# Attention scores from high and low parts, and one filling tile behind every head

## Chip, core and metric

The kernel runs on one core of one Trainium2 chip. The time is the device time of one execution in microseconds (us). Five engines work side by side and meet at semaphores: PE (TensorE: matmul; its weight loads are listed as PEld), DVE (VectorE), ACT (ScalarE), POOL (GpSimd) and SP (SyncE), which here issues the loads of the weights.

## What is computed

Four layers over 512 positions of width 1024, all in float32. Layers 0 and 1 are a retention and convolution block with a feed-forward part; the change does not touch what they do. Layers 2 and 3 are the second block, and the change is in its latent attention:

```python
def mla_attention(c_q, c_kv, k_rope_in, q_norm_g, w_uq, kv_norm_g, w_ukv):
    q = (rmsnorm_2(c_q, q_norm_g) @ w_uq).reshape(B, S, H, 192)      # 8 heads: 128 + 64 rotated
    kv = (rmsnorm_2(c_kv, kv_norm_g) @ w_ukv).reshape(B, S, H, 256)  # keys 128, values 128
    q_nope, q_rope = q[..., :128], rope(q[..., 128:])
    k_nope, v = kv[..., :128], kv[..., 128:]
    k_rope = rope(k_rope_in)                                         # one for all heads
    ...
    s = einsum('bqhd,bkhd->bhqk', qi, k) * scale                     # blocks of 128 queries
    s = where(key_chunk <= q_chunk, s, -1e30)
    p = softmax(s)
    return einsum('bhqk,bkhd->bqhd', p, v)
```

Around it, `y_b = mla_attention(...) * silu(z_b)`, and `merged` is the sum of `sigmoid(g) * (y @ w_proj)` over three branches, of which attention is b.

## The kernel before

A weight chunk, mostly 128 x 1024, is loaded by SP into one of four buffers (`raw`), ACT casts it to fp32r as the high part (L896), and DVE subtracts to get the low part (L1313); `slot(name)` on ACT and DVE cuts the chunk that stands two behind `name` in the list made by `plan()`. A product with a weight is then three fp32r matmuls (`three`: high x high, high x low, low x high), and a `tile` is eight such triples of 512 columns, so 24 matmuls into one of eight PSUM banks. Most of the kernel is such tiles. All matmuls are issued by the helper `mm`, line 448, so the views tell them apart by their operands: `h`, `r` are fp32r tiles in the arena, `wh`, `wl` the parts of a weight, `f` are float32 tiles, `ct` the constants.

Each engine has a program of its own, in `build`, and runs it in order. In `mixer2(L)` (L = 2, 3) PE's order is: the tiles ckv1, kr, zb0, the rotation of the keys (`rotate(L, 4)`), zb1, zb2; the rotated channels of the queries, qr0 and qr1, with the rotations between; the values vb0 and vb1; and then the heads. Small steps (`BESIDE`) are tied to the slots of ckv1 and the four chunks behind it: the two norms of the latent vectors. `heads(h)` makes the query part qn (9 matmuls) and the key part kn (6) of head h and then one filling tile: zb3 to zb7 for h = 0 to 4, none for h = 5, gateb_0 and gateb_1 for h = 6 and 7 (these two keep their banks until the projection of branch b). The order written out is

```python
heads(0); scores(0)
for h in range(8):
    if h < 7: heads(h + 1)
    turn(h)                  # ten transposes of the probabilities
    if h < 7: scores(h + 1)
    values(h)
```

`scores(h)` works in float32: for i = 0 to 3 the 128 queries of block i against 128 (i + 1) keys, one matmul over the 128 plain channels and one over the 64 rotated ones (upper or lower half of the partitions by the head). ACT copies qn out of PSUM (`copied`, L977) and DVE kn (L1687), two buffers each. Behind the scores DVE masks (L1700), takes the maximum (L1702), ACT takes the exponentials (L1167), DVE scales (L1712); PE turns the probabilities (L795), ACT (L1177) and DVE (L1720) copy them, and `values(h)` multiplies in float32. DVE multiplies by the gate (L1727), ACT and DVE split the result (L970, L1323). The rotation is POOL's (`cosine` L1921, `roped` L1926) and DVE's (`rotated` L1537). Behind the heads come the v tiles (va, 192 matmuls) and the projection of branch b with its gates (`gate_proj`).

Of the kernel before, what the change touches and what calls it, by code (L numbers as in the profile page):

```python
# [43 lines left out]
def plan():  # L44
# [43 lines left out]
    for l in range(2):  # L88
# [10 lines left out]
        for h in range(3):  # L99
            one("zb", D2["zb"], h)  # L100
# [6 lines left out]
        for h in range(8):  # L107
            out.append((f"{L}/qk{h}", [("mla_w_uq_2", l, k * P, P, rng(h * 192)) for k in range(3)]
                        + [("mla_w_ukv_2", l, k * P, P, rng(h * 256)) for k in range(2)]))
            if h < 5:  # L110
                one("zb", D2["zb"], h + 3)
            elif h > 5:
                one("gateb_", D2["gate"] + 1024, h - 6)

        def proj(nm, w, nk, b):
            if nm != "b":
                one(f"gate{nm}_", D2["gate"] + 1024 * b, 0)
            for j in range(8):
                if j < 7 and (nm, j) != ("b", 0):
                    one(f"gate{nm}_", D2["gate"] + 1024 * b, j + 1)  # L120
# [69 lines left out]
ZB_AT = (20, 21, 22, 23, 29, 30, 31, 67)  # L190
# [122 lines left out]
ROPE_T = {0: (64, 65, 66, 67), 1: (64, 65, 66, 68, 57)}  # L313
# [6 lines left out]
def build(nc, x_in, wst, vec, cst, tab, gmb, gains_in, out):  # L320
    ctx = ExitStack()
    with ctx:
# [52 lines left out]
        def turned(key):  # L375
            return bank(key).rearrange("p (k s) -> p k s", k=4)

# [57 lines left out]
        def tensor(e, w):  # L435
# [292 lines left out]
            def mixer2(L):  # L728
# [6 lines left out]
                tile(f"{L}/zb2", xs)  # L735
# [26 lines left out]
                def heads(h):  # L762
# [6 lines left out]
                    if h < 5:  # L769
                        tile(f"{L}/zb{h + 3}", xs)  # L770
                    elif h > 5:
                        tile(f"{L}/gateb_{h - 6}", xs, hold=True)

                def scores(h):
                    part = slice(64 * (h % 2), 64 * (h % 2) + 64)
                    qn, kn = F(55 + 2 * (h % 2)), F(56 + 2 * (h % 2))
                    w.wait_ge(*at("qn", L, h))
                    w.wait_ge(*at("kn", L, h))
                    w.wait_ge(*at("roped", L, 3))
                    w.wait_ge(*at("roped", L, 4))  # L780
                    for i in range(NT):
                        n = (i + 1) * P
                        o = take(("s", L, h, i))
                        mm(o[:, 0:n], qn[:, i * P:n], kn[:, 0:n], True, False)
                        mm(o[:, 0:n], F(43 + h // 2)[part, i * P:n], F(42)[part, 0:n], False, True).then_inc(
# [22 lines left out]

                heads(0)
                scores(0)  # L810
                for h in range(8):
                    if h < 7:
                        heads(h + 1)
                    turn(h)
                    if h < 7:
                        scores(h + 1)
                    values(h)
# [17 lines left out]
                banks.let_go(f"{L}/gateb_0")  # L835
                banks.let_go(f"{L}/gateb_1")
                gate_proj(L, "b", "b", "b", pair(16, 24, 8), ("b_lo", L), first=2)
# [44 lines left out]
        def scalar(e, w):  # L882
# [144 lines left out]
            def gate_proj(L, b, g, p, first=0, kind="one", cut_merged=None):  # L1027
                if first == 0:
                    slot(f"{L}/gate{g}_0")
                ring = (66, 67, 68) if L < 2 else (46, 47, 48) if b == "b" else (64, 65, 66)  # L1030
                for j in range(8):
# [6 lines left out]
                    key = f"{L}/gate{g}_{j}"  # L1038
                    w.wait_ge(*at("done", key))
# [1132 lines left out]
```

## Time and profile before

| | |
|---|---|
| three timed runs | 3335.03, 3328.9, 3334.95 us |
| their median | 3334.95 us |
| the profiled execution | 3340.64 us |
| its span, first to last instruction | 3339.3 us |
| PE busy | 3287.9 us (98%) |
| DVE, ACT, POOL busy | 1797.3, 1211.4, 374.6 us |
| mean granted TensorE clock | 0.992 |

Times in rows are from the span's start. Matmuls overlap in the pipeline, so their listed durations are longer than the pace at which they come; the pace is read from the starts. A float32 matmul shows as two instructions, an fp32r one as one. The first scores of layer 2 start at 1772.59 us, and its v tiles at 1915.85; in layer 3 these are 2596.8 and 2741.6.

### The profile page before, as it was taken

Reading aid. Unit: us, or ns where it says so; the run is one execution under the profiler, and the core shown is the slowest. Engines: PE = TensorE matmul, PEld = TensorE weight load, DVE = VectorE, ACT = ScalarE, POOL = GpSimd, SP = SyncE. Lnnn points to the kernel's source line nnn. Section 1 sums busy time; section 2 is a strip of 40 time slices with the busy share of each in tenths; the row PEclk is TensorE's granted clock in tenths of the full one; section 3 lists DMA queues with packets and bytes.
Section 4 is the critical chain, followed back from the end, with each engine's and each line's share of the span. In section 5 each row is a group of like instructions: output and inputs, shape, how many; then the busy total and the mean of one; then the engine's idle time right before and its main releaser. Section 6 shows DMA issues by size and latency. Waiting matters only on the chain.

```text
span 3339.3 us, 36641 instructions
## 1 busy us (share of the span) xinstructions
PE 3287.9 (98%) x14952; PEld 2674.4 (80%) x14952; DVE 1797.3 (54%) x2349; ACT 1211.4 (36%) x1800; POOL 374.6 (11%) x292
## 2 busy tenths in 40 slices
PE   8999999999999999999999999999999999999999
PEld 7788888888878888788886588888888668888887
DVE  4785556665478455666554443447554444344754
ACT  3232334444323233334443322236534322223742
POOL 1111211110111111111020000110012000011001
PEclk9999999999999999999999899999999989999999
DMA  4223222245322322324521132223232122222232
GB/s 157 70 81 103 95 95 95 95 146 189 121 69 80 104 90 93 101 95 148 190 92 49 63 102 88 95 88 98 92 123 78 53 69 89 94 95 90 86 104 96
DMA packets 93638, 330.84 MB, mean 99 GB/s; under 512 B 10560, under 2 KB 10816, under 8 KB 92704
## 3 DMA queue, kind: packets, MB, share of 16 engines
q1 hardware_dynamic: 90144, 313.90, 28.0%
q0 software_dynamic: 3328, 14.59, 1.3%
q8 instruction: 120, 1.97, 0.2%
q14 instruction: 46, 0.38, 0.0%
HBM read 326.35 MB, written 2.10 MB: 98 GB/s over the span
## 4 chain that ended last, share of the span: by engine, by line
PE 94%; DVE 3%; ACT 1%; issue 1%; POOL 0%; DMA 0%; SPq 0%; ACTq 0%; DVEq 0%; POOLq 0%
PE ps L448 93%; DVE wl L1313 1%; ACT wh L896 1%; PE ps L553 1%; PE ps L795 0%; DVE f L1607 0%; DVE X L1423 0%; DMA raw<-wst 0%; ACT f L1167 0%; ACT r L970 0%; DVE f L1420 0%; DVE f L1367 0%; POOL f L1985 0%; DVE f L1712 0%; DVE f L1432 0%
## 5 line engine op out<-in xcount | busy, mean ns | idle before, releaser
L448 PE MATMUL ps<-h,wh 128*128 128x512 f32 (+1 forms) x5824 | 1711.2, 378 | 11.9 <-issue 7.5
L448 PEld LDWEIGHTS ps<-h,wh 128*128 128x128 f32 x5824 | 1070.7, 189 | 213.7 <-issue 19.6
L448 PE MATMUL ps<-h,wl 128*128 128x512 f32 (+1 forms) x2912 | 1095.8, 376 | 0.0
L1313 DVE TENSOR_TENSOR wl<-raw,wh 128x1024 fp32r<-128x1024 f32 (+3 forms) x592 | 740.5, 1265 | 377.7 <-ACT wh L896 376.5
L896 ACT CAST wh<-raw 128x1024 fp32r<-128x1024 f32 (+3 forms) x596 | 593.7, 1009 | 735.5 <-PE ps L448 726.1
L448 PEld LDWEIGHTS ps<-h,wl 128*128 128x128 f32 x2912 | 551.1, 189 | 99.9
L448 PE MATMUL ps<-r,wh 128*128 128x512 f32 x1632 | 506.8, 392 | 1.2 <-DVE f L1367 1.2
L448 PEld LDWEIGHTS ps<-r,wh 128*128 128x128 f32 x1632 | 305.1, 188 | 68.5 <-issue 6.4
L448 PE MATMUL ps<-r,wl 128*128 128x512 f32 x816 | 317.8, 389 | 0.0
L448 PE MATMUL ps<-wh,r 128*128 128x512 f32 x960 | 304.7, 392 | 0.3
L970 ACT CAST r<-f 128x512 fp32r<-128x512 f32 x182 | 111.9, 620 | 515.4 <-DVE f L1616 145.9
L1524 DVE TENSOR_TENSOR f<-f,ps 128x512 f32<-128x512 f32 x96 | 65.9, 686 | 386.6 <-PE ps L448 384.3
L448 PEld LDWEIGHTS ps<-wh,r 128*128 128x128 f32 x960 | 180.2, 188 | 39.9 <-ACT r L896 1.9
L448 PE MATMUL ps<-f,f 128*128 128x128 f32 (+7 forms) x640 | 201.8, 450 | 7.6 <-DVE f L1687 4.3
L1955 POOL TENSOR_TENSOR f<-f,f 128x512 f32<-128x512 f32 x64 | 114.4, 1790 | 752.4 <-DVE f L1524 752.4
L448 PEld LDWEIGHTS ps<-f,f 128*128 128x128 f32 (+1 forms) x640 | 106.2, 198 | 105.8 <-issue 80.1
L448 PE MATMUL ps<-wl,r 128*128 128x512 f32 x480 | 186.8, 389 | 0.0
L1323 DVE TENSOR_TENSOR r<-f,r 128x512 fp32r<-128x512 f32 x182 | 124.6, 690 | 115.5 <-ACT r L970 115.4
L448 PEld LDWEIGHTS ps<-r,wl 128*128 128x128 f32 x816 | 153.1, 188 | 32.2
L1337 DVE SCALAR_TENSOR_TENSOR f<-f,vt,f 128x511 f32<-128x511 f32 (+29 forms) x240 | 174.5, 788 | 0.0
L1607 DVE SCALAR_TENSOR_TENSOR f<-ps,vt,f 128x511 f32<-128x511 f32 (+1 forms) x176 | 131.2, 747 | 64.3 <-ACT f L1104 61.2
L448 PE MATMUL ps<-wh,h 128*128 128x512 f32 x384 | 122.3, 397 | 0.0
(142 smaller groups left out, 2133.7 us busy)
## 6 DMA issues: line engine op xcount, KB each, us to landing
raw<-wst SPq DMA_DIRECT2D x544, 512.0 KB, 3.3
raw<-wst SPq DMA_DIRECT2D x48, 320.0 KB, 3.0
f<-gains POOLq DMA_DIRECT2D x6, 1024.0 KB, 5.2
raw<-wst SPq DMA_DIRECT2D x16, 384.0 KB, 3.1
f<-tab POOLq DMA_DIRECT2D x16, 256.0 KB, 4.2
X<-x_in SPq DMA_DIRECT2D x4, 512.0 KB, 7.7
f<-gmb POOLq DMA_DIRECT2D x4, 512.0 KB, 4.6
raw<-wst SPq DMA_DIRECT2D x8, 256.0 KB, 2.9
```

The lines of the kernel that those rows point to most:

```text
L448: return e.matmul(o, a, b, start=start, stop=stop, skip_group_check=True)
L553: last = e.transpose(o[:, i * P:(i + 1) * P], F(H[a])[:, i * P:(i + 1) * P], ident)
L896: e.copy(h[:, 0:WIDTH[c]], raw[:, c % NRAW, 0:WIDTH[c]]).then_inc(*hi_cut.up(("hi", c)))
L970: e.copy(r, f).then_inc(*act_hi.up(event))
L1313: e.tensor_tensor(l[:, 0:WIDTH[c]], raw[:, c % NRAW, 0:WIDTH[c]], h[:, 0:WIDTH[c]].bitcast(F32), ALU.subtract).then_inc(*lo_cut.up(("lo", c)))
L1323: e.tensor_tensor(lo, f, hi.bitcast(F32), ALU.subtract).then_inc(*dve_lo.up(event))
L1337: e.scalar_tensor_tensor(out=C, in0=F(16 + j)[:, 0:S - s], scalar=vec1(L, "cfw", 31 * j + i)[:, 0:1], in1=C, op0=ALU.mult, op1=ALU.add).th ...
L1524: e.tensor_tensor(F(M + j) if begins else q, q, bank(key), ALU.mult).then_inc(*dve_tile.up(("free", key), *events))
L1607: e.scalar_tensor_tensor(out=q[:, s:S], in0=bank(key)[:, 0:S - s], scalar=vec1(L, "fcw", 3 * (22 * m + j) + 2 - s)[:, 0:1], in1=q[:, s:S], ...
L1955: e.tensor_tensor(F(M + j), F(M + j), F(ring[j % 3]), ALU.add).then_inc(*pool_sum.up(*events))
```

## The change

- The scores: ACT casts qn and kn to fp32r (55 and 57), DVE subtracts for the low parts (56 and 58), one buffer each. For the plain channels PE does `three`. The rotated queries of a head are kept with the high part in the head's own 64 partitions and the low part in the other 64 of one tile; the rotated keys have the same 64 channels in both halves, so one matmul over 128 rows gives high x high and low x high, and one over 64 rows gives high x low. Five fp32r matmuls take the place of two float32 ones.
- ACT and DVE split the rotated parts: one cast and one subtraction for the keys, two each of 64 partitions for every one of the four query tiles. POOL leaves the rotated result in place.
- The filling tiles: zb2 leaves the place ahead of the queries, heads 0 to 4 are followed by zb2 to zb6, heads 5 to 7 by gateb_0 to gateb_2, and zb7 is split: six of its eight triples ahead of the last turning and two ahead of the last values. ACT takes the sigmoid of gateb_0 at head 5. The norm's last step moves with its slot to qr0.

The diff, cut to its core (the same moves of zb and gateb chunks in `plan()` and in each engine's program left out):

```diff
-ZB_AT = (20, 21, 22, 23, 29, 30, 31, 67)
+ZB_AT = (17, 26, 19, 28, 29, 30, 31, 67)
+QR_AT = ((43, 16), (44, 18), (45, 20), (46, 22))
+KR_AT = (42, 23)
...
 # tensor, mixer2
                 for p in range(2):
+                    slot(f"{L}/qr{p}")
                     h, l = weights(f"{L}/qr{p}")
...
                     if h < 5:
-                        tile(f"{L}/zb{h + 3}", xs)
-                    elif h > 5:
-                        tile(f"{L}/gateb_{h - 6}", xs, hold=True)
+                        tile(f"{L}/zb{h + 2}", xs)
+                    else:
+                        tile(f"{L}/gateb_{h - 5}", xs, hold=h > 5)
...
                 def scores(h):
                     part = slice(64 * (h % 2), 64 * (h % 2) + 64)
-                    qn, kn = F(55 + 2 * (h % 2)), F(56 + 2 * (h % 2))
+                    qr, (kr_h, kr_l) = R(QR_AT[h // 2][h % 2]), (R(i) for i in KR_AT)
                     w.wait_ge(*at("qn", L, h))
                     w.wait_ge(*at("kn", L, h))
-                    w.wait_ge(*at("roped", L, 3))
-                    w.wait_ge(*at("roped", L, 4))
+                    w.wait_ge(*at("rope_lo", L, 4, 0))
+                    w.wait_ge(*at("rope_lo", L, h // 2, h % 2))
                     for i in range(NT):
                         n = (i + 1) * P
+                        b = slice(i * P, n)
                         o = take(("s", L, h, i))
-                        mm(o[:, 0:n], qn[:, i * P:n], kn[:, 0:n], True, False)
-                        mm(o[:, 0:n], F(43 + h // 2)[part, i * P:n], F(42)[part, 0:n], False, True).then_inc(
+                        three(o[:, 0:n], R(55)[:, b], R(56)[:, b], R(57)[:, 0:n], R(58)[:, 0:n], True, False)
+                        mm(o[:, 0:n], qr[:, b], kr_h[:, 0:n], False, False)
+                        mm(o[:, 0:n], qr[part, b], kr_l[part, 0:n], False, True).then_inc(
                             *group_done.up(("done", ("s", L, h, i))))
...
+                def last_gate(some):
+                    name = f"{L}/zb7"
+                    h, l = weights(name)
+                    if some[0] == 0:
+                        take(name)
+                    last = group(bank(name), h, l, [k * P for k in some], [xs[k] for k in some], some[0] == 0, some[-1] == 7)
+                    if some[-1] == 7:
+                        last.then_inc(*group_done.up(("done", name), ("closed", NAME[name])))
...
                 for h in range(8):
                     if h < 7:
                         heads(h + 1)
+                    else:
+                        last_gate(range(0, 6))
                     turn(h)
                     if h < 7:
                         scores(h + 1)
+                    else:
+                        last_gate(range(6, 8))
                     values(h)
 # scalar, mixer2
+                def rope_hi(r):
+                    w.wait_ge(*at("roped", L, r))
+                    t = F(ROPE_T[1][r])
+                    if r == 4:
+                        e.copy(R(KR_AT[0]), t).then_inc(*act_hi.up(("rope_hi", L, 4, 0)))
+                        return
+                    for m in range(2):
+                        part = slice(64 * m, 64 * m + 64)
+                        e.copy(R(QR_AT[r][m])[part, :], t[part, :]).then_inc(*act_hi.up(("rope_hi", L, r, m)))
...
                 def heads(h):
                     slot(f"{L}/qk{h}")
-                    more = (at("done", ("s", L, h - 2, 3)),) if h > 1 else ()
-                    copied(("qn", L, h), F(55 + 2 * (h % 2)), ("qn", L, h), *more)
+                    more = (at("done", ("s", L, h - 1, 3)),) if h else ()
+                    hi_part(bank(("qn", L, h)), R(55), at("done", ("qn", L, h)), ("qn_hi", L, h), *more)
+                    hi_part(bank(("kn", L, h)), R(57), at("done", ("kn", L, h)), ("kn_hi", L, h))
...
+                    if h == 5:
+                        key = f"{L}/gateb_0"
+                        w.wait_ge(*at("done", key))
+                        e.activation(gate_at(L, "b", 0), bank(key), ACT.Sigmoid).then_inc(
+                            *act_tile.up(("gate", L, "b", 0), ("free", key)))
 # vector, mixer2
+                def rope_lo(r):
+                    t = F(ROPE_T[1][r])
+                    if r == 4:
+                        lo_part(t, R(KR_AT[0]), R(KR_AT[1]), at("rope_hi", L, 4, 0), ("rope_lo", L, 4, 0))
+                        return
+                    for m in range(2):
+                        part, other = slice(64 * m, 64 * m + 64), slice(64 - 64 * m, 128 - 64 * m)
+                        q = R(QR_AT[r][m])
+                        lo_part(t[part, :], q[part, :], q[other, :], at("rope_hi", L, r, m), ("rope_lo", L, r, m))
...
                 def heads(h):
                     slot(f"{L}/qk{h}")
-                    key = ("kn", L, h)
-                    w.wait_ge(*at("done", key))
-                    if h > 1:
-                        w.wait_ge(*at("done", ("s", L, h - 2, 3)))
-                    e.tensor_copy(F(56 + 2 * (h % 2)), bank(key)).then_inc(*dve_tile.up(("kn", L, h), ("free", key)))
+                    for nm, hi in (("qn", 55), ("kn", 57)):
+                        key = (nm, L, h)
+                        w.wait_ge(*at(nm + "_hi", L, h))
+                        e.tensor_tensor(R(hi + 1), bank(key), R(hi).bitcast(F32), ALU.subtract).then_inc(
+                            *dve_lo.up((nm, L, h), ("free", key)))
...
 # gpsimd
             def roped(L, r, dst):
...
-                e.tensor_tensor(F(dst), F(dst), F(ROPE_T[L // 2][r]), ALU.add).then_inc(*pool_tile.up(("roped", L, r)))
+                t = F(ROPE_T[L // 2][r])
+                e.tensor_tensor(F(dst) if L < 2 else t, F(dst), t, ALU.add).then_inc(*pool_tile.up(("roped", L, r)))
```

On ACT, `rope_hi(4)` stands in the query loop behind the slot of qr1, and `rope_hi` of query tiles 0 and 1 behind the copies of vb0, of 2 and 3 behind those of vb1; on DVE `rope_lo` likewise.

## Rows read from the trace of the kernel before

**Rows 1.** The page's fourth part: the chain that ended last, by engine.

```profile
PE 94%; DVE 3%; ACT 1%; issue 1%; POOL 0%; DMA 0%; SPq 0%; ACTq 0%; DVEq 0%; POOLq 0%
```

**Rows 2.** Windows: length, then PE, PEld, DVE, ACT, POOL busy, granted clock, DMA.

```profile
1741.12:1763.74 22.62, 22.62 (x93) 17.28 (x92) 7.86 (x9) 10.41 (x16) 11.71 (x8) 1.00 0.22 75
1806.42:1824.42 18.00, 18.00 (x75) 12.09 (x74) 9.21 (x22) 6.28 (x16) 0.00 (x0) 1.00 0.16 48
1857.30:1870.18 12.88, 12.88 (x24) 5.18 (x25) 3.25 (x12) 2.14 (x8) 0.00 (x0) 0.60 0.12 41
1907.98:1911.59 3.61, 1.90 (x10) 1.19 (x11) 2.83 (x6) 1.38 (x3) 0.00 (x0) 0.85 0.65 263
1911.59:1915.85 4.26, 4.26 (x8) 2.44 (x9) 0.00 (x0) 0.00 (x0) 0.00 (x0) 0.50 0.01 4
1915.85:1960.16 44.31, 44.31 (x194) 36.65 (x194) 11.27 (x11) 12.71 (x16) 0.00 (x0) 0.98 0.30 95
2681.50:2695.97 14.47, 14.47 (x25) 5.94 (x25) 3.49 (x13) 2.15 (x8) 0.00 (x0) 0.53 0.11 36
```

**Rows 3.** Timeline of PE: start, length, operation; the first score block and one head.

```profile
1772.59 5.84 PE L448 MATMUL ps<-f,f 128*128 128x128 f32 x16
1778.36 0.73 PE L448 MATMUL ps<-r,wh 128*128 128x512 f32 x2
...
1805.34 1.25 PE L795 MATMUL ps<-ct,f 128*128 128x128 f32 x10
1806.42 8.20 PE L448 MATMUL ps<-f,f 128*128 128x128 f32 x24
1814.38 0.70 PE L448 MATMUL ps<-r,wh 128*128 128x512 f32 x2
```

**Rows 4.** PE's waits, 1709 to 1987 us: who for whom, total, times, longest.

```profile
PE ps L448 <- DVE f L1687: 2.2, 1, 2.2
PE ps L448 <- DVE f L1720: 1.6, 1, 1.6
PE ps L795 <- DVE f L1712: 1.5, 1, 1.5
```

**Rows 5.** Timeline of the weight loads: two changes of rows, then the values.

```profile
1789.78 0.29 PEld L448 LDWEIGHTS ps<-f,f 64*128 64x128 f32 x2 [0.33 <-issue]
...
1794.20 0.30 PEld L448 LDWEIGHTS ps<-f,f 128*128 128x128 f32 x2 [0.76 <-issue]
...
1795.17 1.27 PEld L448 LDWEIGHTS ps<-f,f 128*128 128x128 f32 x5 [0.24 <-issue]
```

**Rows 6.** Timeline of PE: fp32r matmuls of 256 and of 512 columns.

```profile
1707.49 0.40 PE L448 MATMUL ps<-h,wh 128*128 128x256 f32 x2
...
1707.85 0.40 PE L448 MATMUL ps<-h,wh 128*128 128x256 f32 x2
...
1758.08 0.62 PE L448 MATMUL ps<-wh,r 128*128 128x512 f32 x2
...
1758.76 0.62 PE L448 MATMUL ps<-wh,r 128*128 128x512 f32 x2
```

**Rows 7.** Timeline of the weight loads in layer 0: fp32r ahead of 64 rows.

```profile
120.86 0.19 PEld L448 LDWEIGHTS ps<-h,wl 128*128 128x128 f32 x1
121.40 0.29 PEld L448 LDWEIGHTS ps<-f,f 64*128 64x128 f32 x2 [0.35 <-issue]
```

**Rows 8.** Timeline of DVE behind a score block that ends at 1812.2.

```profile
1815.82 1.28 DVE L1712 TENSOR_SCALAR f<-f,sm 128x128 f32<-128x128 f32 x4
...
1818.38 0.69 DVE L1323 TENSOR_TENSOR r<-f,r 128x512 fp32r<-128x512 f32 x1 [0.69 <-ACT r L970]
...
1819.75 0.68 DVE L1687 COPY f<-ps 128x512 f32<-128x512 f32 x1
```

**Rows 9.** Timelines of ACT and of PE around the first rotation.

```profile
1737.95 1.28 ACT L970 CAST r<-f 128x512 fp32r<-128x512 f32 x2 [1.68 <-DVE f L1381]
...
1745.20 0.59 PE L448 MATMUL ps<-f,ct 128*128 128x512 f32 x1
```

More of the change, by code:

```diff
@@ L98, in plan @@
         out.append((f"{L}/kr", [(A, l, k * P, P, rng(D2["kr"], 64)) for k in range(8) for _ in range(2)]))
-        for h in range(3):
+        for h in range(2):
             one("zb", D2["zb"], h)
@@ L110, in plan @@
             if h < 5:
-                one("zb", D2["zb"], h + 3)
-            elif h > 5:
-                one("gateb_", D2["gate"] + 1024, h - 6)
+                one("zb", D2["zb"], h + 2)
+            else:
+                one("gateb_", D2["gate"] + 1024, h - 5)
+        one("zb", D2["zb"], 7)
         def proj(nm, w, nk, b):
@@ L118, in proj @@
             for j in range(8):
-                if j < 7 and (nm, j) != ("b", 0):
+                if j < 7 and (nm != "b" or j > 1):
                     one(f"gate{nm}_", D2["gate"] + 1024 * b, j + 1)
@@ L376, in turned, with gate_at @@
             return bank(key).rearrange("p (k s) -> p k s", k=4)
+        def gate_at(L, b, j):
+            if L < 2:
+                return F(66 + j % 3)
+            if b == "b":
+                return F(68 if j == 0 else 46 + j % 3)
+            return F(64 + j % 3)
         def stat(t):
@@ L834, in mixer2 @@
                                 last.then_inc(*group_done.up(*closes))
-                banks.let_go(f"{L}/gateb_0")
                 banks.let_go(f"{L}/gateb_1")
-                gate_proj(L, "b", "b", "b", pair(16, 24, 8), ("b_lo", L), first=2)
+                banks.let_go(f"{L}/gateb_2")
+                gate_proj(L, "b", "b", "b", pair(16, 24, 8), ("b_lo", L), first=3)
                 for nm in ("u", "za"):
@@ L1184, in mixer2 @@
                         heads(h + 1)
+                    else:
+                        slot(f"{L}/zb7")
                     turn(h)
@@ L1193, in mixer2 @@
                         copied(("va", L, n, t), F(32 + 2 * t, 2)[:, n * S:(n + 1) * S], ("va", L, n, t))
-                gate_proj(L, "b", "b", "b", first=2)
+                gate_proj(L, "b", "b", "b", first=3)
                 for nm in ("u", "za"):
@@ L1735, in mixer2 @@
                         heads(h + 1)
+                    else:
+                        slot(f"{L}/zb7")
                     turn(h)
@@ L1745, in mixer2 @@
                         slot(f"{L}/va{n_}_{c}")
-                gate_proj(L, "b", "b", "b", first=2)
+                gate_proj(L, "b", "b", "b", first=3)
                 for nm in ("u", "za"):
```

57 lines of the change are left out of this document (34 added, 23 removed).

## The prediction

> **What bounds the kernel now.** First the page's chain of work, which gives 94% of the span of 3339.3 us to PE [rows 1]. TensorE is nearly never without work, so only what shortens TensorE's own stream, or its few pauses, moves the end. The profiled execution took 3340.64 us (1.3 us lie outside its span); the three timed runs have a median of 3334.95 and reach from 3328.9 to 3335.03.
>
> Second, the timeline of PE in one attention stage. A head is one period: score matmuls, values, the projections of the next head, a filling tile, the turning of the probabilities; it lasts 18.00 us from one score block to the next [rows 2], with no pause. The first head's score block stands alone, from 1772.59 to 1778.36: 5.77 us. Scores and values together go from 1806.42 to 1814.38, 7.96 us, so values take 2.19; ten transposes take 1.09 (1805.34 to 1806.42) [rows 3].
>
> Third, PE's waits from 1709 to 1987 us. Three pauses of the stage stand there: 2.15 us before head 5's scores (until the copy of line 1687), 1.54 before the last head's turning (until the scaling of line 1712), 1.64 before its values (until the copy of line 1720) [rows 4]. They are the three places without a filling tile: heads(5) has none, and behind head 7 there is nothing left. The windows show what follows a pause: TensorE's granted clock is 1.00 in the ordinary head, a mean of 0.60 over the scores that follow the 2.15 us pause and 0.50 over the last values, which is the lower level, 1.2 GHz [rows 2].
>
> **The score block.** Before, each of a head's four score tiles (128, 256, 384, 512 columns, 1280 together) is two fp32 matmuls, one over 128 rows and one over 64; each shows as two instructions. After, it is five fp32r matmuls, four over 128 rows and one over 64. What does a column cost? The values are fp32 over 128 rows with the same 1280 columns and take 2.19 us with about 0.05 us of change at their ends, so two such sets stream for 4.27. The block takes 5.77, and 1.50 are left over for its eight changes between 128 and 64 rows: 0.19 each. The weight loads show the same: within the values the loads run on beneath the matmuls, while at each change the next load comes only after a gap of its own (0.33 us at 256 columns, 0.76 at 512), which is the streaming of the matmul before it and more [rows 5].
>
> An fp32r matmul of 512 columns comes every 0.227 us (three from 1758.08 to 1758.76), one of 256 columns every 0.120 (three from 1707.49 to 1707.85) [rows 6]. 384 columns lie between them: 0.174. For 128 columns no row shows fp32r. From below stands what the two widths extrapolate to, 0.067; from above the fp32 rate of four passes, 0.21. I take 0.112, since the transposes, which also load 128 columns of weights for each 128 streamed, come every 0.109 [rows 3]. Does the change from 128 to 64 rows also cost an fp32r stream? In layer 0 the last 128-row fp32r load starts at 120.86; at the pace of 0.227 the next would start at 121.09, beneath its matmul. That next one is of 64 rows and starts at 121.40 [rows 7]: the matmul has streamed its 512 columns by 121.30, and the load comes 0.1 us after that, uncovered. So I keep 0.19 for each of the eight changes; the bound below is zero (the load beneath the stream), the bound above 0.21 (0.1 of waiting and the 0.11 that the next load takes uncovered).
>
> New block: for each tile three steps at the sustained pace and two bare streams (before a change nothing is pushed on). 3 x (0.227 + 0.174 + 0.120 + 0.112) = 1.90; 2 x 1280 columns at 0.417 ns (2.13 us of the values over their 4 x 1280) = 1.07; 8 x 0.19 = 1.51. Sum 4.48 us against 5.77: 1.29 a head, **20.7 us** for 16 heads (two layers).
>
> The Trainium skill speaks for more: TensorE: Matmul & The Clock Gate, section "Step-by-step: what each phase is for", says that weight loads are pulled ahead of running matmuls if the row groups don't conflict or if they go to the background buffer. By it, a change of rows need cost nothing and the block would be 2.97 us, the whole gain 24 us larger. The trace agrees within one row count and not across a change [rows 5, 7].
>
> **The fillers.** Moving tiles changes no work: 24 matmuls each, before as after. zb2 goes from ahead of the queries to head 1, each later one a head on, gateb_0 to 2 behind heads 5 to 7, and zb7 is split 18 + 6 around the last turning. The pauses: 2.15 + 1.54 + 1.64 = 5.33 us a layer. What the lower clock adds in layer 2: scores and values of head 5 in 12.88 instead of 7.96 (4.92), the window of the last turning 3.61 less the pause of 1.64 at its end and the ordinary 1.09 (0.88), the last values 4.26 less 2.19 (2.07), the v stage 44.31 less 192 x 0.227 = 43.58 (0.73) [rows 2]: 8.60. In layer 3 the block of head 5 took 14.47 (6.51 over), 1.6 more: 10.2. Together 5.33 x 2 + 8.6 + 10.2 = **29.5 us**, if the fillers cover the pauses.
>
> Do they? From a score block's end (1812.2) its probabilities are ready at 1817.1 (four scalings, 1815.82 to 1817.10) [rows 8], 4.9 us. Behind heads 0 to 6 lie the values and, 18.00 - 7.96 - 1.09 = 8.95, the projections and a filler: 11.1. Behind head 7 lie 2.19 and 18 x 0.227 = 4.09: 6.3, enough. The last values then need the copies of line 1720: DVE has the product and the lower part of head 6 (1818.38 + 0.69, 6.9 us behind the block) and now also the cut of va0_1, 1.2; that and 0.7 for the copy give 9.0; PE arrives at 6.3 + 1.09 + 6 x 0.227 = 8.7. I charge **0.3 us** a layer.
>
> **New waits.** (1) Scores wait for low parts in place of copies: ACT casts two tiles a head (0.64 each, two in 1.28 [rows 9]) where it copied one, then DVE subtracts twice (0.69, as at 1818.38) where it copied once (0.68) [rows 8]. The copy of before ended at 1820.43 and the scores began at 1824.42: 4.0 us of room; the added 0.69, and up to 0.6 behind the second cast, leave 2.7. Queued behind are the next cut, the gate's product and the copy of the turned tile, all at least 2 us early. Cost nothing; without that cover up to 1.3 us a head. (2) The rope parts: nine casts and nine subtractions a layer, 0.6 to 0.7 each, about 6 us on ACT and on DVE, in the 22.6 us of the query and value projections, where ACT is busy for 10.4 and DVE for 7.9 [rows 2]. GpSimd writes in place, no more work. On ACT the last four stand ahead of head 0's casts; scores(0) come 8.8 us behind the last value tile (39 matmuls), and four casts, two more and two subtractions make 2.5 + 1.3 + 0.7, beside a cut of 1.0. Nothing. (3) With zb2 gone, TensorE reaches the first rotation one tile (5.5 us) sooner: at 1739.7, not 1745.2. That needs ACT's copy, which stands behind the two casts of the second norm, ended at 1739.23 [rows 9], pushed by a weight cut that is 1024 wide now and not 768 (0.2 to 0.4 more), and takes 0.6: 1740.2. PE waits **0.6 us** a layer; a bare queue of casts bounds it at 1.2, below at zero. (4) The sigmoid of gateb_0 stands among exponentials: ACT switches its table twice more a layer. ACT's idle time before head 5's exponentials covers both. Weight chunks stay in number; SP's queue has the same transfers in another order, TensorE consuming them 7% faster at the most; no PE wait in rows 4 is for a transfer.
>
> **Sum.** 20.7 + 29.5 - 2 x (0.3 + 0.6) = 48.4 us. Against the profiled time: 3340.6 - 48.4 = 3292.2; against the median: 3286.5. The profiled run was 5.7 above the median, and the length of the low-clock stretch differs between its own two layers by 1.6 us; part of that excess I expect to be what now goes away. I take **3288 us**.
>
> **Rivals.** A, 128 columns of fp32r run at the fp32 rate: five of them 1.07 instead of 0.44, 0.63 a head, 10 us: 3298. No row speaks against it. B, the loads at a change of rows run ahead once both sides are fp32r, and the change costs nothing: 1.51 a head more gained, 24 us: 3264. For it: within one row count every load is hidden [rows 5]; against it: an fp32r stream of 128 rows did not let the 64-row load ahead [rows 7]. (It is what the Trainium skill's rule above would give.) C, the clock falls in the new blocks: streaming is 2.67 of 4.48 us, before 4.27 of 5.77, so TensorE works less densely there, next to the turning. At 1.2 GHz such a block takes 2.7 us more; in half of the heads 21 us, 3310; in all, 3331, still not above before. For it: it fell after pauses in this very place; against it: no ordinary head shows it. D, a filler does not cover (the low parts arrive late in each head): 1.3 us a head and the pauses half kept, 3320. E, on the other side: fp32r with 64-row operands, or narrower than 512, is streamed at the fp32 rate in the score tiles altogether: five matmuls of four passes, 5 x 2.13 + 1.51 = 12.2 us a block, 6.4 more than before, 102 us: 3334.95 + 102 - 27.7 = 3409. It decides from a block of 7.5 us on (48.4 / 16 = 3.0 above 4.48). Against it: the 256-column rows. That the change does not do what it says would be D.
>
> **Chances.** Forecast 0.66, A 0.12, B 0.07, C 0.08 (3310), D 0.04, E 0.03. Range: 3264 to 3306 holds the forecast, A, B and the milder half of C; D, E, the rest of C and some 0.08 for sizes that I missed, 0.19 together, stay out. Within 0.2% (6.7 us) of before, which is about what a measurement of this kernel can tell from no change, lie only the ends of C and D: 0.02; slower: E and the unseen, 0.03; faster 0.95.
>
> **What would show it.** Period of a head 18.00 -> 16.7; the lone first block 5.77 -> 4.5; the loads at a change of rows still with a gap; no granted clock under 1.00 between the first scores and the v stage; PE's waits at lines 1687, 1712, 1720 gone, one of some 0.6 us for the ACT copy ahead of the first rotation and one of 0.3 ahead of the last values. A step under 0.1 us between the 128-column matmuls, or over 0.2, would correct the estimate; a low clock inside the heads would make the prediction wrong.

## The result, and the profile after

The changed kernel takes 3309.76 us, the median of four runs from 3306.52 to 3310.53; the kernel before beside it takes 3334.99 (3328.9 to 3337.31). The ratio is 0.9925, with a 95% interval of 0.9908 to 0.9942: faster by 25 us, where 47 were forecast. The forecast was 3288 with a range from 3264 to 3306; the time lies 3.8 us above the range. The direction was right, the size wrong. The profiled execution of the changed kernel took 3310.41 us.

The page of the kernel after, its head and its fourth part:

```profile
span 3309.1 us, 36837 instructions
PE 3258.3 (98%) x15016; PEld 2684.7 (81%) x15016; DVE 1820.3 (55%) x2383; ACT 1234.7 (37%) x1838; POOL 375.2 (11%) x292
...
PE 95%; DVE 2%; ACT 1%; issue 1%; POOL 0%; DMA 0%; SPq 0%; ACTq 0%; DVEq 0%; POOLq 0%
```

PE still sets the end, as in [rows 1]. Its waits from 1709 to 1987 us in the kernel after, in the columns of [rows 4]:

```profile
PE ps L461 <- issue: 4.6, 1, 4.6
PE ps L461 <- ACT f L1006: 0.9, 2, 0.5
```

The three pauses of [rows 4] are gone, and so is the lower clock behind them. In their place stands one pause of 4.6 us, more than any of the three, and its releaser is "issue": the profile names no one. Of the two waits for the ACT copy one (0.52 us) was there before, the other (0.42) is new. The timeline of PE shows where they stand: the first score block, one head, the new wait ahead of the first rotation, and the big pause.

```profile
1742.98 1.10 PE L461 MATMUL ps<-f,ct 128*128 128x512 f32 x2 [0.42 <-ACT f L1006]
...
1783.97 1.26 PE L810 MATMUL ps<-ct,f 128*128 128x128 f32 x10
1784.98 4.70 PE L461 MATMUL ps<-r,r 128*128 128x128 f32 x20
1789.61 2.42 PE L461 MATMUL ps<-f,f 128*128 128x512 f32 x8
1791.79 0.71 PE L461 MATMUL ps<-r,wh 128*128 128x512 f32 x2
...
1800.73 1.25 PE L810 MATMUL ps<-ct,f 128*128 128x128 f32 x10
...
1949.92 1.19 PE L461 MATMUL ps<-r,wh 128*128 128x512 f32 x2 [4.63 <-issue]
```

A head is now 16.76 us long (1783.97 to 1800.73) instead of 18.00; its score block takes 4.63 (1784.98 to 1789.61) instead of 5.77, its transposes 1.01 instead of 1.09. The pause ends at 1949.92, at the first matmul of branch b's projection (`gate_proj`), behind the v tiles. The windows of the kernel after, in the columns of [rows 2]: a head, the v tiles with the pause, and the first two tiles of the projection; then these last two again in layer 3.

```profile
1790.00:1806.77 16.77, 16.77 (x78) 12.84 (x77) 9.69 (x23) 6.77 (x16) 0.00 (x0) 1.00 0.16 51
1901.50:1949.92 48.42, 43.79 (x195) 35.98 (x194) 14.23 (x17) 17.07 (x21) 0.09 (x1) 0.98 0.28 91
1949.92:1963.43 13.51, 13.51 (x49) 10.90 (x49) 7.01 (x10) 1.05 (x1) 2.98 (x2) 0.80 0.18 64
...
2710.04:2758.49 48.45, 43.82 (x196) 35.97 (x194) 14.24 (x17) 17.07 (x21) 0.10 (x1) 0.99 0.28 91
2758.49:2772.19 13.70, 13.70 (x48) 11.03 (x49) 7.00 (x10) 1.05 (x1) 2.98 (x2) 0.79 0.18 64
```

The 48 matmuls behind the pause would take 48 x 0.227 = 10.9 us at the full clock; they take 13.5 and 13.7 at a mean granted clock of 0.80. The pause and what follows it cost (4.63 + 2.63) + (4.63 + 2.82) = 14.7 us. That alone carries most of the distance to the forecast. The question for the experiments is what PE waits for there.

What stands in front of PE's first projection matmul is its wait for a PSUM bank. The eight banks go round in a ring (`Banks.take`): each take gets the next bank that isn't held, and waits until the tile that had it is read ("free"). Counted through the code, take by take, in layer 2:

| take | before: bank, last tile in it | after: bank, last tile in it |
|---|---|---|
| held while the v tiles run | 1 (gateb_0), 5 (gateb_1) | 1 (gateb_1), 5 (gateb_2) |
| zb7, behind head 7 | none | 0 |
| last v tile | 7 | 0 |
| first projection tile, pr(b, 0) | 0, a v tile read long ago | 1, **gateb_1** |
| the next tile | 1, gateb_0 | 2, a v tile |

The held banks are let go just ahead of `gate_proj`. Before, the ring stood at bank 0 then. zb7 is one take more, the ring stands one bank further, and the first projection tile gets bank 1, which is free only when ACT has taken the sigmoid of gateb_1. ACT's timeline in the kernel after shows when:

```profile
1945.33 0.58 ACT L1006 COPY f<-ps 128x512 f32<-128x512 f32 x1 [0.77 <-PE ps L461]
1945.81 1.99 ACT L925 CAST wh<-raw 128x1024 fp32r<-128x1024 f32 x2
1947.82 1.28 ACT L1070 ACT_TABLE_LOAD   x1
1949.11 0.60 ACT L1070 ACTIVATE f<-ps 128x512 f32<-128x512 f32 x1
```

The sigmoid ends at 1949.71 and PE's next weight load starts at 1949.89. It stands behind the last copy of a v tile, two cuts of weight chunks (1.99) and a change of ACT's table (1.28). PE would have gone on at 1945.29.

A note on the table: the Trainium skill, ScalarE: Activation LUTs, section "What ACT_TABLE_LOAD costs", counts 1.28 us for the load and 1.38 more for a drain. The trace agrees with the first; of the second it shows nothing, since the cut ends 0.02 us before the load and the sigmoid starts 0.01 behind it. Read from the rows, the sigmoid in this place costs 1.9 us with its table.

### The profile page after: what moved, and what is told of

Its sections match the earlier page's. It is cut to its first block, busy times and chain, and to the rows that moved or that the text cites. A ratio compares the mean times of both kernels' runs of the same rounds, so it can differ in the third digit from the quotient of the medians.

```text
span 3309.1 us, 36837 instructions
## 1 busy us (share of the span) xinstructions
PE 3258.3 (98%) x15016; PEld 2684.7 (81%) x15016; DVE 1820.3 (55%) x2383; ACT 1234.7 (37%) x1838; POOL 375.2 (11%) x292
## 4 chain that ended last, share of the span: by engine, by line
PE 95%; DVE 2%; ACT 1%; issue 1%; POOL 0%; DMA 0%; SPq 0%; ACTq 0%; DVEq 0%; POOLq 0%
PE ps L461 94%; DVE wl L1367 1%; ACT wh L925 1%; PE ps L566 1%; PE ps L810 1%; DVE f L1661 0%; DVE X L1477 0%; DMA raw<-wst 0%; DVE f L1474 0%; DVE f L1421 0%; POOL f L2059 0%; DVE f L1486 0%; ACT r L999 0%; DVE f L1424 0%; ACT f L957 0%
## 5 line engine op out<-in xcount | busy, mean ns | idle before, releaser
L1377 DVE TENSOR_TENSOR r<-f,r 128x512 fp32r<-128x512 f32 (+1 forms) x200 | 140.7, 708 | 117.8 <-ACT r L999 115.4
L461 PE MATMUL ps<-r,r 128*128 128x512 f32 (+5 forms) x800 | 189.2, 376 | 0.0
L461 PEld LDWEIGHTS ps<-r,wl 128*128 128x128 f32 x816 | 154.3, 189 | 32.9
L461 PEld LDWEIGHTS ps<-r,r 128*128 128x128 f32 (+1 forms) x800 | 139.8, 188 | 39.4 <-issue 12.8
```

The costliest lines, as they stand in the source:

```text
L461: return e.matmul(o, a, b, start=start, stop=stop, skip_group_check=True)
L1377: e.tensor_tensor(lo, f, hi.bitcast(F32), ALU.subtract).then_inc(*dve_lo.up(event))
```

## Experiments

The theory: the pause is the bank, the lower clock follows from the pause, and the rest of the forecast holds. The rival: the pause belongs to the fp32r scores or their low parts, which keep DVE and ACT behind. Each kernel was timed beside the kernel before on the same chip; its median there is given in brackets.

### The held banks kept longer

In the changed kernel the two banks are let go two projection tiles later, so that pr(b, 0) takes a bank whose v tile has been read:

```diff
 # tensor, gate_proj
                 for j in range(8):
+                    if b == "b" and j == 2:
+                        banks.let_go(f"{L}/gateb_1")
+                        banks.let_go(f"{L}/gateb_2")
...
-                banks.let_go(f"{L}/gateb_1")
-                banks.let_go(f"{L}/gateb_2")
                 gate_proj(L, "b", "b", "b", pair(16, 24, 8), ("b_lo", L), first=3)
```

> The changed kernel with one difference: TensorE's program keeps the two held banks of gateb_1 and gateb_2 until the third projection of branch b, so the first projection takes a bank whose v tile was copied long before. Theory (bank): the 4.6 us pause behind the v tiles is the wait for the bank of gateb_1, which ACT's sigmoid frees; it goes, and with it the low clock behind it: v tiles 48.4 -> 43.6 us, the first three groups behind them 13.5 -> 10.9, 7.5 us a layer, about 15 in all, so some 3295 us. Rival (weights): the pause waits for the weight chunks of prb_0; it stays at 4.6 us and the time at 3310. Rival (clock moves on): the pause goes but the clock falls somewhere else near, and only 9.3 us come back: 3300.

Measured: 3295.14 us (before 3337.84), ratio 0.9871 [0.9856, 0.9886]. Windows of this kernel, the v tiles and the two projection tiles behind them, and its ACT timeline:

```profile
1901.13:1944.78 43.65, 43.65 (x195) 36.13 (x194) 11.28 (x11) 12.71 (x16) 0.00 (x0) 1.00 0.28 97
1944.78:1955.66 10.88, 10.88 (x49) 9.02 (x48) 8.51 (x14) 5.41 (x6) 1.54 (x1) 1.00 0.20 59
```
```profile
1945.46 1.99 ACT L926 CAST wh<-raw 128x1024 fp32r<-128x1024 f32 x2
1947.48 1.28 ACT L1071 ACT_TABLE_LOAD   x1
1948.77 0.60 ACT L1071 ACTIVATE f<-ps 128x512 f32<-128x512 f32 x1
```

ACT does exactly the same, and as late: its sigmoid ends at 1949.37, 4.6 us after PE has gone on at 1944.78. Nobody waits for it any more. The v tiles take 43.65, the tiles behind them 10.88, at a clock of 1.00, and no stretch of lower clock is left from about 1697 us to the last microseconds. 14.6 us against the changed kernel, with the same instructions in the same order and only other banks: the pause is the bank. The expectation's other rival, weight chunks that come late, falls too: ACT casts the same two chunks just as late, from 1945.46, and PE has gone on before.

### The sigmoid ahead of the cuts

The other way to release the bank sooner. On ACT, in `gate_proj` of branch b:

```diff
 # scalar, gate_proj
+                def gate(j):
+                    key = f"{L}/gate{g}_{j}"
...
+                    e.activation(gate_at(L, b, j), bank(key), ACT.Sigmoid).then_inc(
+                        *act_tile.up(("gate", L, b, j), ("free", key)))
+                if b == "b":
+                    gate(1)
                 for j in range(8):
...
-                    if (b, j) != ("b", 0):
...
+                    if (b, j) not in (("b", 0), ("b", 1)):
+                        gate(j)
```

> The changed kernel with one difference: ACT takes the sigmoid of gateb_1 ahead of the two weight cuts (1.05 us each) that stood before it. Theory (bank): the pause is the sum of the last v copy, two cuts, the table load of 1.28 and the sigmoid of 0.6; without the cuts it shrinks from 4.6 to about 2.5 us, and 4.2 us come back in two layers, or up to 9 if the clock no longer falls: 3301 to 3306. Rival (weights): cutting later makes the pause longer, 4.6 -> 6.5 us, and the kernel slower, 3314.

Measured: 3303.85 us (before 3337.84), 0.9898 [0.9883, 0.9913]. ACT's timeline, then PE's, of this kernel:

```profile
1943.56 0.58 ACT L1006 COPY f<-ps 128x512 f32<-128x512 f32 x1 [0.77 <-PE ps L461]
1944.16 1.28 ACT L1063 ACT_TABLE_LOAD   x1
1945.46 0.60 ACT L1063 ACTIVATE f<-ps 128x512 f32<-128x512 f32 x1
```
```profile
1946.26 1.01 PE L461 MATMUL ps<-r,wh 128*128 128x512 f32 x2 [2.74 <-issue]
```

The pause moves with the sigmoid: it ends 0.2 us behind it again, and is shorter by nearly the two cuts (4.63 to 2.74 us, and the cuts take 1.99). It gives 5.9 us where the pauses alone are 3.8 shorter; the clock still falls, for a shorter stretch (the 48 matmuls take 12.58). Price and place of the mechanism are confirmed from a second side.

### The two halves of the change alone

First the fp32r scores with the filling tiles left where they were (diff: the changed kernel with the moves of the zb and gateb chunks undone).

> The fp32r scores with the filling tiles where they were before (zb2 ahead of the queries, none behind head 5, none behind head 7). By the prediction's own term: the score block goes from 5.77 to 4.6 us and the transposes from 1.09 to 1.01, 1.2 us a head, 19 to 20 us less than before, about 3315; the three pauses of a layer stay, and the first projection does not pause, since its bank is that of a v tile. If the scores feed less than that (a rival in which the fillers carried the gain), 3325 or more. The pause ahead of head 5's scores grows by about the extra cast and subtraction, 1.3 us at most, a layer.

Measured: 3315.12 us (before 3337.84), 0.9931 [0.9917, 0.9946], 22.7 us faster. The waits of PE from 1709 to 1987 us in this kernel, and the scores and values of head 5 in layer 2 and layer 3 as windows:

```profile
PE ps L460 <- DVE r L1731: 2.7, 1, 2.7
PE ps L460 <- DVE f L1765: 1.6, 1, 1.6
PE ps L809 <- DVE f L1757: 1.5, 1, 1.5
```
```profile
1854.10:1865.45 11.35, 11.35 (x29) 6.95 (x29) 3.59 (x13) 2.14 (x8) 0.00 (x0) 0.55 0.10 38
2668.42:2676.66 8.24, 8.24 (x29) 5.19 (x29) 3.08 (x10) 0.95 (x5) 0.00 (x0) 0.79 0.15 54
```

No pause stands ahead of the projection, although the scores are fp32r and the low parts are there: the rival falls. Where no filler covers, the low part's subtraction makes the pause 0.55 us longer than in [rows 4] (2.70 against 2.15), less than the 0.69 and up to 0.6 more that the prediction put there without cover. And the same place costs 11.35 us in one layer and 8.24 in the other, against 6.81 (4.63 + 2.18) in an ordinary head: how long the clock stays low behind a pause of one and the same length differs.

Then the filling tiles moved, with the scores left in float32 (diff: the kernel before with these moves, the split of zb7, and the sigmoid of gateb_0 at head 5).

> The kernel before with the new places of the filling tiles alone; the scores stay in fp32. Theory: the three pauses and the low clock behind them go (29.5 us), the bank pause of the changed kernel comes with its low clock (15 us), and the first rotation waits 0.4 us a layer: 14 us less than before, about 3321. If the bank pause belonged to the fp32r scores and not to the order of the tiles, there would be none here and the time 3306.

Measured: 3326.51 us, the median of seven runs (before 3337.84), 0.9966 [0.9955, 0.9978], 11.3 us faster. Windows of this kernel, v tiles and the two projection tiles:

```profile
1908.20:1956.62 48.42, 43.79 (x195) 35.98 (x194) 14.24 (x17) 17.07 (x21) 0.09 (x1) 0.98 0.28 91
1956.62:1969.78 13.16, 13.16 (x49) 10.70 (x49) 7.02 (x10) 1.05 (x1) 2.98 (x2) 0.82 0.18 68
```

The pause of 4.63 us is all here, with float32 scores. It belongs to the order of the tiles. By the medians the kernel is 11.3 us faster and not the 14 that were expected; between the two profiled executions (3340.64 and 3326.51 us) it is 14.1. The same kernel with the banks held as in the first experiment:

> The kernel before with the new places of the filling tiles and the held banks kept until the third projection; scores in fp32. The fillers' own worth without the bank pause. The prediction had 29.5 us for the pauses and the low clock, less 0.6 a layer: 28 us less than before. The kernel with fillers alone was 11.3 us under before and has two pauses of 4.6 us with low clock behind them (7.1 us a layer): with them gone, 25 us less than before. Below 20 the pauses would have been worth less than their length.

Measured: 3314.3 us (before 3338.48), 0.9928 [0.9913, 0.9943], 24.2 us faster, and by the medians 12.2 below the kernel without the held banks. Its windows of the same two stretches:

```profile
1913.91:1957.55 43.64, 43.64 (x196) 36.13 (x195) 11.27 (x11) 12.71 (x16) 0.00 (x0) 1.00 0.29 97
1957.55:1968.43 10.88, 10.88 (x50) 9.01 (x49) 8.51 (x14) 5.41 (x6) 1.54 (x1) 1.00 0.19 56
```

So by the medians the moved tiles are worth 24 us by themselves, and about half of that was lost again to the bank.

### What a change of rows costs

The prediction's biggest assumption in the block was 0.19 us for each of eight changes between 128 and 64 rows. Two kernels take changes away. In the first the last score matmul runs over all 128 rows, so no change is left (it adds low x low of the rotated channels):

```diff
-                        mm(o[:, 0:n], qr[part, b], kr_l[part, 0:n], False, True).then_inc(
+                        mm(o[:, 0:n], qr[:, b], kr_l[:, 0:n], False, True).then_inc(
```

> The changed kernel with the last matmul of each score tile over all 128 rows in place of 64 (it then adds low x low of the rotated channels as well, a term that the 64-row form leaves out). Theory (change of rows costs): eight changes a head go, the block falls from 4.63 to 3.2 us (five fp32r matmuls at 0.112, 0.120, 0.174 and 0.227), 1.45 us a head, 23 us in all: 3287 from 3310. Rival (the width costs, not the change of rows): the block stays over 4 us and the time within 5 us of the changed kernel. The bank pause behind the v tiles stays in both.

Measured: 3285.61 us (before 3338.48), 0.984 [0.9826, 0.9855], 24 us below the changed kernel. One head in its PE timeline:

```profile
1797.28 1.25 PE L810 MATMUL ps<-ct,f 128*128 128x128 f32 x10
1798.29 3.44 PE L461 MATMUL ps<-r,r 128*128 128x128 f32 x20
1801.57 2.32 PE L461 MATMUL ps<-f,f 128*128 128x512 f32 x8
1803.64 0.71 PE L461 MATMUL ps<-r,wh 128*128 128x512 f32 x2
```

The block is 3.28 us (1798.29 to 1801.57) with the same count of matmuls and columns, the values behind it 2.07 instead of 2.18. Its pause ahead of the projection is still 4.63 us. One wait is new, 0.24 us ahead of the last values in each layer: the DVE copy of the turned probabilities ends at 1887.18 us there, and PE's next weight load starts at 1887.26.

In the second, the four 64-row matmuls stay, but stand together behind the other sixteen, so that two changes are left of eight. The banks are held here, so it is compared with the first experiment:

```diff
                         mm(o[:, 0:n], qr[:, b], kr_h[:, 0:n], False, False)
-                        mm(o[:, 0:n], qr[part, b], kr_l[part, 0:n], False, True).then_inc(
+                    for i in range(NT):
+                        n = (i + 1) * P
+                        b = slice(i * P, n)
+                        mm(bank(("s", L, h, i))[:, 0:n], qr[part, b], kr_l[part, 0:n], False, True).then_inc(
                             *group_done.up(("done", ("s", L, h, i))))
```

> The changed kernel with held banks kept, and the four 64-row matmuls of a head behind one another after all sixteen of 128 rows, so two changes of rows a head in place of eight; the same matmuls. Theory (each change costs 0.19 us): the block falls from 4.63 to about 3.5 us and the time from 3295 to some 3277. Rival (a 64-row matmul is slow by itself): the block stays at 4.6 and the time at 3295.

Measured: 3278.78 us (before 3338.48), 0.9821 [0.9807, 0.9836], against 3295.14 for the ungrouped one. Its block in the PE timeline and the weight loads at the end of it; last, from the changed kernel, the loads around one change:

```profile
1796.85 3.62 PE L461 MATMUL ps<-r,r 128*128 128x128 f32 x20
1800.40 2.42 PE L461 MATMUL ps<-f,f 128*128 128x512 f32 x8
...
1889.11 2.17 PE L461 MATMUL ps<-f,f 128*128 128x512 f32 x6 [1.16 <-DVE f L1793]
```
```profile
1799.57 0.52 PEld L461 LDWEIGHTS ps<-r,r 64*128 64x128 f32 x4 [0.36 <-issue]
```
```profile
1805.96 0.18 PEld L461 LDWEIGHTS ps<-r,r 64*128 64x128 f32 x1 [0.36 <-issue]
1806.39 0.30 PEld L461 LDWEIGHTS ps<-f,f 128*128 128x128 f32 x2 [0.25 <-issue]
```

Six changes fewer make the block 3.55 us instead of 4.63: 0.18 each. Two left cost 3.55 - 3.28 = 0.27, so 0.14 each. Grouped, the four 64-row loads follow each other with one gap in front of them; ungrouped, each has a gap of its own. This answers what the prediction drew from the Trainium skill's rule on weight loads (TensorE: Matmul & The Clock Gate, "Step-by-step: what each phase is for"), that a change of rows need cost nothing. In these traces weight loads run ahead within 128 rows and within 64 rows, and not from one to the other, for fp32r no more than for float32. Grouping also makes a new wait of 1.16 us in each layer, ahead of the last values: the DVE copy of the turned probabilities is late. All four score tiles are complete only at the end of the block then, so DVE starts later on the first three. That reading wasn't tested.

Both best parts together, no change of rows and the banks held:

> Both at once: the held banks kept until the third projection, and the last score matmul over 128 rows (with the low x low term of the rotated channels). If the two causes are apart and nothing new is late, 3295 - 23 = 3272 us. If the shorter score block uncovers a copy of the turned probabilities ahead of the values, or lets the clock fall, part of the 23 us is given back: over 3278.

Measured: 3270.11 us (before 3338.48), 0.9797 [0.9781, 0.9814], the fastest kernel here. A stretch of one head's length as a window, and a score block:

```profile
1796.00:1811.31 15.31, 15.31 (x79) 12.70 (x78) 9.70 (x23) 6.76 (x16) 0.00 (x0) 1.00 0.16 56
1795.05:1798.33 3.28, 3.28 (x24) 3.06 (x23) 2.71 (x8) 0.81 (x2) 0.00 (x0) 1.00 0.20 80
```

The two gains add: 3309.76 - 14.6 - 24.2 = 3271. A shorter block leaves less cover for the probabilities, and the wait of 0.24 us ahead of the last values stands here too, about what the prediction charged there for the changed kernel. The profile puts it down to "issue", but the DVE copy of the turned probabilities ends at 1883.94 us and PE's next weight load starts at 1884.02, as in the kernel above.

### The same kernels once more

What had the lower clock cost before? The prediction took 18.8 us from one execution. Two more profiles of the kernel before and one of the kernel after:

> The kernel before, unchanged, profiled a second time. The prediction took the low-clock stretches of one execution as given (scores and values of head 5 in 12.88 and 14.47 us, 4.9 and 6.5 over the ordinary 7.96; 18.8 us of low clock in all). If they are a property of the kernel, this profile shows them within 1 us again. If they depend on the execution, one of the two blocks is shorter by 3 us or more, and the term was taken from a long one.

> The kernel before once more, for the same question: are the two blocks of head 5 again 12.9 and 14.5 us, or do they differ from execution to execution? The pauses themselves (2.15, 1.54, 1.64 us a layer) should be the same to 0.05 us in each.

> The changed kernel, unchanged, profiled a second time: the pause behind the v tiles is 4.63 us in both layers again, and the three groups behind it take 13.2 to 13.5 us if the clock falls there each time, or 10.9 if it does so by chance.

Measured: before 3340.71 and 3335.99 us, after 3306.78. The scores and values of head 5 as windows: layer 2 in the second execution of before, layer 2 in the third, layer 3 in the third.

```profile
1857.46:1870.34 12.88, 12.88 (x24) 5.18 (x25) 3.24 (x12) 2.14 (x8) 0.00 (x0) 0.60 0.12 41
```
```profile
1858.29:1866.31 8.02, 8.02 (x24) 3.71 (x25) 3.03 (x10) 0.94 (x5) 0.00 (x0) 1.00 0.18 65
```
```profile
2677.18:2691.58 14.40, 14.40 (x25) 5.97 (x25) 3.15 (x11) 2.14 (x8) 0.00 (x0) 0.53 0.11 36
```

The pause ahead of these blocks is the same each time (2.15 to 2.17 us). Of the other two pauses of a layer the first is 1.54 each time, and the last 1.63 to 1.64, but 1.42 in layer 2 of the third execution, so not within the 0.05 that were expected. In one of these four places (two executions, two layers) the clock did not fall behind it, the block took 8.02 us instead of 12.88, and that execution was 4.7 us shorter. It fits the way in which the runs of the kernel before differ: of 25 timings 10 lie from 3339.9 to 3344.0, 13 from 3334.7 to 3338.5, and two at 3328.9. The last would have no fall at head 5 in either layer (3340.7 - 4.9 - 6.5 = 3329.3); that is worked out, no profile caught one. The second execution of after has the pause of 4.63 us again in both layers; the 48 matmuls behind the one in layer 2 took 12.98 instead of 13.51.

The executions also differ in layers 0 and 1, which the change does not touch. PE's first wait for an ACT copy in layer 2 (0.52 us in every kernel) ends at 1709.25, 1709.44 and 1710.21 us in the three profiles of before, at 1711.89 and 1709.18 in the two of after, at 1711.58 in the changed kernel with the banks held, and at 1714.52 in the moved tiles alone with the banks held. The clock does part of this. One stretch of layer 1, in the first profile of before and in the first of after, shows 16 matmuls at a granted clock of 1.00 and 9 at 0.50:

```profile
1351.20:1354.40 3.20, 3.20 (x16) 2.65 (x15) 3.16 (x4) 0.75 (x2) 0.00 (x0) 1.00 0.66 186
1351.20:1354.40 3.20, 3.20 (x9) 2.53 (x8) 3.17 (x4) 0.76 (x2) 0.00 (x0) 0.50 0.50 175
```

What the change did is therefore read better from that wait to the end. In the same order: before, after, the changed kernel with the banks held, and the moved tiles alone with the banks held.

```profile
1709.25:3339.34 1630.09, 1607.66 (x7076) 1279.21 (x7076) 778.95 (x1112) 596.69 (x924) 151.79 (x110) 0.99 0.26 87
1711.89:3309.11 1597.22, 1575.46 (x7140) 1286.91 (x7140) 803.30 (x1146) 619.85 (x962) 152.45 (x110) 1.00 0.27 89
1711.58:3293.63 1582.05, 1569.54 (x7140) 1283.45 (x7140) 803.50 (x1146) 619.76 (x962) 152.51 (x110) 1.00 0.27 90
1714.52:3316.14 1601.62, 1589.05 (x7076) 1271.56 (x7076) 778.96 (x1112) 601.88 (x928) 151.54 (x110) 1.00 0.26 89
```

Against this profile of before, in which the clock fell at head 5 in both layers, the changed kernel gains 32.9 us there, with the banks held 48.0, and the moved tiles alone 28.5.

## Why the prediction was wrong

**What bounds the kernel**: right. PE sets the end before and after, and what was gained or lost shows on PE alone.

**Moving tiles**: here is the step that failed, "Moving tiles changes no work". It is true, and not enough: each tile also takes a place in the ring of banks, and zb7, moved behind the last head, shifts every take behind it by one. The list of new waits went through queues (ACT, DVE, POOL, SP) and left out banks. The wait that it missed costs 4.63 us of pause and 2.6 to 2.8 us of lower clock in each layer, 14.6 us in all by the first experiment (15.2 from the first wait of layer 2 to the end). The trace of before had the pieces: a cast, a table load of 1.28 and a sigmoid on ACT at the start of the projection. Only the order of the takes was needed beside it.

**The fillers' gain**: mechanism right. All three pauses are gone, and no lower clock is left between the first scores and the end of the v tiles. From the first wait of layer 2 to the end it is worth 28.5 us against the 27.7 forecast (29.5 less the two charges), compared with the execution from which the forecast was made. By the medians it is 24.2. Two things can make up the difference: its profiled execution lost 5.3 us ahead of that wait, and the 8.6 and 10.2 us of lower clock are those of an execution in which the clock fell at head 5 in both layers, which it doesn't always. How much each has in the medians is not shown.

**From the profiled time to the median**: this follows from the same fact, and the step from 3292.2 to 3288 went the wrong way. An execution of before with fewer falls is shorter, and has as much less to gain. The time of the changed kernel has no such fall in it, so 3340.6 less 48.4 was the forecast for any execution: 3292.2. Taking a value towards 3286.5 counted the falls twice. With the banks held the kernel takes 3295.1, 2.9 us from that sum; its profiled execution had lost 2.3 us ahead of the first wait of layer 2, and behind it gained 48.0 against the 48.4 forecast.

**The score block**: 4.63 us against 4.48; the lone one 4.54 (from 1770.45 to 1774.99). So the sixteen blocks were 2.2 us dearer than forecast. The transposes behind them, 0.08 shorter each time (1.01 against 1.09, 1.3 us in all), were not foreseen, and the new waits were 1.0 us cheaper, so that the sum came out right with its errors against each other. Within the block the forecast had 2.97 us for streams and pairs and 0.19 for each change of rows. Without any change the block measures 3.28, and against that a change costs 0.17. By the forecast's own split it is (4.63 - 2.97) / 8 = 0.21, its upper bound: it took 0.19 from float32, where it was counted against matmuls at their ordinary pace, and set it beside bare streams. [rows 7], its ground for keeping 0.19 in fp32r, shows a 64-row load that is float32, behind an fp32r stream. The gain by the scores alone was 22.7 us by the medians against 20.7 forecast; its one profiled execution has the transposes shorter and shorter stretches of low clock at head 5 (blocks of 11.35 and 8.24 us in place of 12.88 and 14.47).

**The new waits that were listed**: the first rotation waits 0.42 us, against 0.6; the last values do not wait, against 0.3; the low parts cost nothing in a head. All in their places, each slightly dearer in the forecast.

**The rivals**: A, 128 columns of fp32r at the float32 rate, is out: the whole block without changes of rows is 3.28 us, 5 x (0.227 + 0.174 + 0.120 + 0.112) = 3.17, so that its narrow tiles hold the forecast's pace within 0.11 us together. B, the changes for nothing, is refuted by the grouped kernel. C did not occur: heads run at a granted clock of 1.00. D named a filler that does not cover; all cover. (Its price of 3320 lies between what its terms give with 3288 and 16 x 1.3: 3314 with half of the pauses alone, 3324 with half of what the clock adds too.) E is far off. The measured time is close to C's 3310 by chance, with another mechanism.

The terms, for the profiled execution after: 1.14 x 14 + 1.23 x 2 = 18.4 for the blocks, 29.5 for the three pauses and the clock behind them, 1.3 for the transposes, less 0.84 for the two rotation waits, 15.0 for the bank (the v tiles and the two tiles behind them, 48.42 + 13.51 and 48.45 + 13.70, against 43.65 + 10.88 with the banks held) and 2.6 that all that stands ahead of layer 2's latent attention took longer in this execution (the first wait that ends at 1711.89 us and not at 1709.25): 30.8, against 3340.64 - 3310.41 = 30.2 measured.

## What to carry to other kernels

A tile that moves takes its buffer's turn with it: where buffers go round in a ring, write down the order of takes behind the change, and for the first tile of each later stage ask who had that buffer and when it is released. A wait shown as "issue" at the start of a tile is worth that question. A clock penalty read from one execution is one value of several until more have been seen, and it is not to be taken off a forecast that already contains its end. Where stages that a change does not touch differ between executions, compare from a common point behind them. And put matmuls of the same number of rows together, or pad them to the same rows: it was worth 1.1 to 1.4 us a score block here, as much as the change to fp32r itself.

## What the runs showed of the hardware

- Going between 128-row and 64-row operands on TensorE cost 0.14 to 0.18 us each time with fp32r, against a block at its ordinary pace (eight cost 4.63 - 3.28 = 1.35 us, two 0.27). With float32 it was 0.19 by the prediction's working, 1.50 us over eight.
- In the score block without changes of rows, 3.28 us for its 20 matmuls, an fp32r matmul of 128 columns starts about every 0.11 us; one of 512 columns comes every 0.227 [rows 6].
- The granted clock fell to 0.50, the level of 1.2 GHz, behind pauses of 2.15 us in five of the six places seen in the kernel before (three executions, two layers) and behind 2.70 and 2.74 us each time (two places each); behind the 1.16 us of the grouped kernel it did not (two places). How long it stayed low differed between executions of one kernel.
- An ACT table load between two operations cost 1.28 us, with 0.02 us of idle time ahead of it and 0.01 behind.
